# Group norm statistics inside the wkv7 loop, and another order of scores, maxima and norms in the attention of a hybrid decoder layer

## The reference

```
# RWKV-7 branch: 8 heads of 64
y, wkv = wkv7_scan(wkv0, rh, decay, kh, vh, -kk, kk * ah)
mu  = mean(y, axis=-1);  var = mean(square(y - mu), axis=-1)       # per token and head
y = (y - mu) * rsqrt(var + RW_GN_EPS) * rw_ln_w + rw_ln_b
y = y + sum(rh * kh * rw_r_k, axis=-1) * vh                        # the bonus
y = y * g                                                          # g = sigmoid(gd) @ rw_g2

# differential attention: 4 heads, two softmax maps each, causal
p = softmax(where(k_pos <= q_pos, q @ k.T * 64**-0.5, -inf))       # two maps per head
o = (p[map 0] - lam * p[map 1]) @ v
```

## Time and profile before

| | us |
|---|---|
| median of three runs | 2958.01 |
| the profiled execution | 2952.79 |
| its span | 2951.1 |
| TensorE busy (21313 matmuls) | 2745.0, 93% |
| VectorE busy (1339 instructions) | 1361.3, 46% |
| ScalarE busy | 658.3, 22% |
| GpSimd busy | 257.1, 9% |

### The profile page before, as it was taken

The page is one execution under the profiler, slowest core; times in us unless marked ns, Lnnn a source line. Parts: engine busy times, 40 slices in busy tenths (PEclk is TensorE's granted clock), DMA queues, the critical chain, the costliest instruction groups (busy, mean ns, idle before and its releaser), DMA issues.

```text
span 2951.1 us, 51413 instructions
## 1 busy us (share of the span) xinstructions
PE 2745.0 (93%) x21313; PEld 2582.2 (87%) x21313; DVE 1361.3 (46%) x1339; ACT 658.3 (22%) x967; POOL 257.1 (9%) x250
## 2 busy tenths in 40 slices
PE   6999999999999999996776999669999999999998
PEld 6999999999999999993344889439999999999998
DVE  4332233233673788776553656475453322332334
ACT  4111111112311222323322232111221111111123
POOL 1000000000000232111002454100000000000000
PEclk8999999999999999997987999769999999999999
DMA  3111111111333456669534000104211111111112
GB/s 101 50 43 50 43 50 50 43 43 50 115 99 103 143 175 223 201 188 330 164 114 124 25 28 17 42 29 145 92 44 50 50 43 45 48 50 45 48 41 74
DMA packets 270203, 252.02 MB, mean 85 GB/s; under 512 B 20724, under 2 KB 216144, under 8 KB 269920
## 3 DMA queue, kind: packets, MB, share of 16 engines
q1 hardware_dynamic: 252960, 189.42, 21.5%
q0 software_dynamic: 16896, 60.33, 5.6%
q10 hardware_dynamic: 192, 0.07, 0.0%
HBM read 209.87 MB, written 39.90 MB: 85 GB/s over the span
## 4 chain that ended last, share of the span: by engine, by line
PE 85%; DVE 9%; ACT 2%; issue 1%; DMA 1%; SPq 0%; DVEq 0%; POOL 0%; POOLq 0%; ACTq 0%
PE ps L1670 71%; DVE small L1438 1%; ACT probs L1022 1%; PE ps L1974 1%; PE ps L1989 1%; PE ps L1693 1%; PE ps L1994 1%; DVE rstd L1583 1%; PE ps L1714 1%; PE ps L1896 1%; PE ps L2001 1%; PE ps L1911 1%; PE ps L1834 1%; PE ps L2021 1%; PE ps L2029 1%
## 5 line engine op out<-in xcount | busy, mean ns | idle before, releaser
L1670 PE MATMUL ps<-h_hi,w_hi 128*128 128x344 f32 x3072 | 991.7, 323 | 10.3 <-DVE w_lo L1160 10.3
L1670 PE MATMUL ps<-h_lo,w_hi 128*128 128x344 f32 x3072 | 980.6, 319 | 0.0
L1670 PE MATMUL ps<-h_hi,w_lo 128*128 128x344 f32 x3072 | 980.3, 319 | 0.0
L1670 PEld LDWEIGHTS ps<-h_hi,w_hi 128*128 128x128 f32 x3072 | 577.8, 188 | 25.9 <-issue 19.8
L1670 PEld LDWEIGHTS ps<-h_lo,w_hi 128*128 128x128 f32 x3072 | 577.9, 188 | 2.1 <-issue 1.9
L1670 PEld LDWEIGHTS ps<-h_hi,w_lo 128*128 128x128 f32 x3072 | 577.9, 188 | 0.0
L1670 PE MATMUL ps<-ff_hi,w_hi 128*128 128x344 f32 x1056 | 337.1, 319 | 0.0
L1670 PE MATMUL ps<-ff_lo,w_hi 128*128 128x344 f32 x1056 | 336.6, 319 | 0.0
L1670 PE MATMUL ps<-ff_hi,w_lo 128*128 128x344 f32 x1056 | 336.2, 318 | 0.0
L810 ACT ACTIVATE w_hi<-w_stage 128x1024 fp32r<-128x1024 f32 x194 | 203.8, 1051 | 479.9 <-PE ps L1670 479.9
L1160 DVE TENSOR_TENSOR w_lo<-w_stage,w_hi 128x1024 fp32r<-128x1024 f32 x194 | 239.3, 1233 | 139.4 <-ACT w_hi L810 103.8
(11 more groups left out here) (388 smaller groups left out, 3219.1 us busy)
## 6 DMA issues: line engine op xcount, KB each, us to landing
w_stage<-in_ffn_up SPq DMA_DIRECT2D x176, 256.0 KB, 3.1
key_ring<-in_cache_k SPq DMA_DIRECT2D x128, 256.0 KB, 3.0
value_ring<-in_cache_v SPq DMA_DIRECT2D x128, 256.0 KB, 3.0
w_stage<-in_w_in SPq DMA_DIRECT2D x84, 256.0 KB, 3.3
w_stage<-in_ffn_down SPq DMA_DIRECT2D x80, 256.0 KB, 2.9
gate_save<-tmp POOLq DMA_DIRECT2D x16, 516.0 KB, 4.5
gate_ring<-gate_save POOLq DMA_DIRECT2D x16, 516.0 KB, 4.2
row_ring<-row_save SPq DMA_DIRECT2D x40, 128.0 KB, 2.9
```

Source lines behind the costliest of these rows:

```text
L1670: last = mm(dense[s][:, j], w[w0][:, k0 + k, :], r[:, k, j * CH:(j + 1) * CH], start=(k == 0 and n == 0), stop=(k == nk - 1 and n == 2))
```

## The change

**Group norm.** The mean is taken out before the outputs are formed: each of the three left operands of the output sums (state, values, solution) is centred over its 64 columns, so that y comes out centred. Its square is taken at once, and per chunk eight products with two columns of weights give, as token rows of each head, the variance and the bonus sum r k r_k; these are finished on 128 to 136 columns at a time. After the loop one root over all tokens follows, and each double head gets three parts: the two rows spread to 128 partitions, and the gate.

**Attention.** In steps 0 to 15 (n up to 512) the scores of a step use banks 0 and 1 (one map each) or 2 and 3, in turn, so they wait for the exponentials two steps back; VectorE takes the maxima of step s+1 ahead of the norm of step s. In steps 16 to 31 the mask, the maxima and the scaling are done map by map, and ScalarE waits for each map by itself.

```
# constants: one more table, (partition % 32 == column // 64), for the spread of two rows
+    put("row_heads", (s % 32 == t // 64) * 1.0)

# attention
+        def score_at(step, m):
+            return m * 512 + step % 2 * 1024 if step < 4 * HP else m * 1024
# ScalarE, probs(step)
-                act.wait_ge(*ev.at("neg_max", step + 1))
                 if step >= 2:
                     act.wait_ge(*ev.at("o_done", step - 1))
                 for m in range(2):
+                    act.wait_ge(*ev.at("neg_max", 2 * step + m + 1))
+                    b = score_at(step, m)
...
# VectorE, maxima(step)
+                for ms in ((0, 1),) if step < 4 * HP else ((0,), (1,)):
...
             maxima(0)
             for step in range(STEPS):
                 qi, s = step // HP, step % 2
                 n = (qi + 1) * P
+                if step + 1 < 4 * HP:
+                    maxima(step + 1)
                 dve.wait_ge(*ev.at("probs_made", 2 * step + 2))
...
-                if step + 1 < STEPS:
+                if 4 * HP <= step + 1 < STEPS:
                     maxima(step + 1)
# TensorE, scores(step)
-                pe.wait_ge(*ev.at("probs_made", 2 * step))
+                if step >= 2:
+                    pe.wait_ge(*ev.at("probs_made", 2 * step if step >= 4 * HP else 2 * step - 2))

# wkv7 loop: GpSimd, behind first_masks(c)
+            def bonus_products(c):
+                cols = slice(c * C, NT if c == NC - 1 else (c + 1) * C)
...
+                nc.gpsimd.tensor_tensor(Kf[:, :, cols], Rf[:, :, cols], Kf[:, :, cols], ALU.mult).then_inc(ev["ck_rk"], 1)
# ScalarE, behind ck_y
-                    sc.activation(CUM[:, :, p * C:(p + 1) * C], Y_PS, ACT.Copy).then_inc(ev["ck_y_out"], 1)
+                    sc.activation(CUM[:, :, p * C:(p + 1) * C], Y_PS, ACT.Copy)
+                    sc.activation(Bf[:, :, p * C:(p + 1) * C], Y_PS, ACT.Square).then_inc(ev["ck_y_out"], 1)
# VectorE, in next_state(p)
+                if p + 1 < NC:
+                    mean = mean8[:, 0:HP]
+                    in_turn(v.tensor_reduce(mean, new, AX, ALU.add))
+                    in_turn(v.scalar_tensor_tensor(Sc[(p + 1) % 2], mean.unsqueeze(2).broadcast_to([P, HP, 64]), -1.0 / 64, new,
+                                                   ALU.mult, ALU.add).then_inc(ev["ck_sc"], 1))
+            def centred_values(c):
+                dve.wait_ge(*ev.at("ck_tok_moved", 3 * c + 1))
+                in_turn(v.tensor_reduce(mean8, vtok.rearrange("p h (x n) -> p (h x) n", x=2), AX, ALU.add))
+                mean = mean8.rearrange("p (h x) -> p h x", h=HP).unsqueeze(3).broadcast_to([P, HP, 2, 64])
+                in_turn(v.tensor_scalar(mean8, mean8, 1.0 / 64, None, ALU.mult))
+                in_turn(v.tensor_tensor(Bf[:, :, c * C:(c + 1) * C].rearrange("p h (x n) -> p h x n", x=2),
+                                        vtok.rearrange("p h (x n) -> p h x n", x=2), mean, ALU.subtract).then_inc(ev["ck_vc"], 1))
+            def centred_solution(p):      # the same for Us (waits for ck_u_moved), written to KKn
...
+            def token_rows(p):
...
+                dve.wait_ge(*ev.at("ck_rows", p + 1))
+                in_turn(v.tensor_scalar(Rf[:, 0, cols], PS[:, 7, 0:n], 0.0, GN_EPS, ALU.max, ALU.add))
+                in_turn(v.tensor_copy(Rf[:, 1, cols], PS[:, 7, n:2 * n]).then_inc(ev["ck_rows_in"], 1))
+                in_turn(v.reciprocal(Rf[:, 0, cols], Rf[:, 0, cols]).then_inc(ev["y_inverse"], 1))
# VectorE, the loop over c
                 if c < NC:
                     level_sums(c, 1)
+                if c:
+                    centred_solution(p)
+                if c < NC:
                     level_sums(c, 2)
                 if c:
                     next_state(p)
+                    token_rows(p)
...
                     in_turn(v.tensor_tensor(heads8(arb), heads8(ABR_PS), wide("incl"), ALU.mult).then_inc(ev["ck_arb"], 1))
+                    centred_values(c)
# TensorE, outputs(p): reads Sc, the centred values and the centred solution, waits for ck_sc, ck_vc, ck_uc
+            def token_rows(p):
...
+                for h in range(HP):
+                    mm(PS[32 * h:32 * h + 2, 7, 0:n], row_scale, Bf[:, h, cols], start=True, stop=True)
+                for h in range(HP):
+                    last = mm(PS[32 * h:32 * h + 2, 7, n:2 * n], row_bonus[:, h], Kf[:, h, cols], start=True, stop=True)
+                last.then_inc(ev["ck_rows"], 1)
# TensorE, the loop over c
                 lower_products(c, 3)
                 if c + 1 < NC:
                     blocks(c + 1)
+                if c:
+                    token_rows(p)
                 level_products(c, 3)
+                if c:
+                    pe.wait_ge(*ev.at("ck_rows_in", c))
                 turn(c, 0, Vf[:, :, c * C:(c + 1) * C])

# after the loop, ScalarE
+            act.wait_ge(*ev.at("y_inverse", NC))
+            sc.activation(Rf[:, 0, :], Rf[:, 0, :], ACT.Sqrt).then_inc(ev["y_root"], 1)
             for h in range(HP):
...
+                act.wait_ge(*ev.at("y_used", 3 * h + 3))
+                sc.activation(YA[0][:, h, :], CUM[:, h, :], ACT.Copy).then_inc(ev["ya_high"], 1)
# after the loop, VectorE (in place of L1573 to L1593)
+            for h in range(HP):
+                y, t1, part = CUM[:, h, :], T[:, h % 2, :], 3 * h
+                dve.wait_ge(*ev.at("y_parts", part + 1))
+                in_turn(v.scalar_tensor_tensor(ch3(y), ch3(y), param("rw_ln_w", h), dense[part % 2], ALU.mult, ALU.mult)
+                        .then_inc(ev["y_used"], 1))
+                dve.wait_ge(*ev.at("y_parts", part + 2))
+                in_turn(v.tensor_tensor(ch3(t1), ch3(Vf[:, h, :]), dense[(part + 1) % 2], ALU.mult).then_inc(ev["y_used"], 1))
+                in_turn(v.scalar_tensor_tensor(y, y, param("rw_ln_b", h), t1, ALU.add, ALU.add))
+                if h:
+                    ya_low(h - 1)
+                dve.wait_ge(*ev.at("y_parts", part + 3))
+                in_turn(v.tensor_tensor(ch3(y), ch3(y), dense[part % 2], ALU.mult).then_inc(ev["y_used"], 1))
+            ya_low(HP - 1)
# after the loop, TensorE (in place of the column sums)
+            for part in range(3 * HP):
+                h, kind = divmod(part, 3)
+                if part >= 2:
+                    pe.wait_ge(*ev.at("y_used", part - 1))
...
+                q = slice(32 * h, 32 * h + 2)
+                for j in range(NCH):
+                    cols = slice(j * CH, (j + 1) * CH)
+                    if kind < 2:
+                        last = mm(dense[part % 2][:, j], K("row_heads")[q], Rf[q, kind, cols], start=True, stop=True)
+                    else:
+                        last = mm(dense[part % 2][:, j], G2[:, h * P:(h + 1) * P], gd[:, cols], start=True, stop=True)
+                last.then_inc(ev["y_parts"], 1)
```

More of the change, by code:

```diff
@@ L337, in build @@
         Pb = per_head(C + 1)
+        Sc = [per_head(64) for _ in range(2)]
+        mean8 = work(8)
+        row_scale = work(2)
+        row_bonus = work(2 * HP).rearrange("p (h x) -> p h x", h=HP)
         cumx = cum.rearrange("p (c n) -> p c n", c=NC)
@@ L755, in _ @@
             first_masks(0)
+            bonus_products(0)
             for c in range(NC):
@@ L1432, in maxima @@
                 n = (qi + 1) * P
[L1433 removed]
                 dve.wait_ge(*ev.at("scores_done", step + 1))
[L1435 to L1439 removed]
+                for ms in ((0, 1),) if step < 4 * HP else ((0,), (1,)):
+                    a, k = ms[0], len(ms)
+                    b = score_at(step, 0)
+                    scores = PSf[:, b:b + 1024].rearrange("p (m n) -> p m n", n=512)[:, :, 0:n] if k == 2 else \
+                        PSf[:, a * 1024:a * 1024 + n].unsqueeze(1)
+                    diag = scores[:, :, qi * P:n]
+                    in_turn(v.tensor_tensor(diag, diag, K("causal").unsqueeze(1).broadcast_to([P, k, P]), ALU.add))
+                    top = small[:, 24 + 2 * s + a:24 + 2 * s + a + k]
+                    in_turn(v.tensor_reduce(top, scores, AX, ALU.max))
+                    in_turn(v.tensor_scalar(small[:, 16 + 4 * s + a:16 + 4 * s + a + k], top, -SCALE, None, ALU.mult)
+                            .then_inc(ev["neg_max"], k))
             maxima(0)
@@ L1536, in state_step @@
                 if part == 8:
-                    in_turn(v.tensor_reduce(ysam[:, h, :], stm, AX, ALU.add))
+                    in_turn(v.tensor_reduce(ysam[:, h, :], stm, AX, ALU.add).then_inc(ev["y_sample"], 1))
+            in_turn(v.memset(Sc[0], 0.0).then_inc(ev["ck_sc"], 1))
+            in_turn(v.tensor_scalar(row_scale, heads, 1.0 / 64, None, ALU.mult))
+            in_turn(v.tensor_tensor(row_bonus, heads.unsqueeze(1).broadcast_to([P, HP, 2]), bc(param("rw_r_k", 0, HP).unsqueeze(2), 2),
+                                    ALU.mult))
             blocks(0)
@@ L1895, in scores @@
                         w = min(512, n - j)
-                        last = mm(PSf[:, m * 1024 + j:m * 1024 + j + w], Q[q, h, qi * P:n], Kr[q, h, j:j + w],
```

(2 more changed lines are left out.)

120 lines of the change are left out of this document (59 added, 61 removed).

## The result

The changed kernel takes 2967.76 us (median of six runs, 2964.25 to 2968.82) against 2955.88 for the kernel before (six runs, 2950.56 to 2962.52): a ratio of **1.0038**, 95% interval 1.0023 to 1.0053. It is slower by about 0.4%, just over what a measurement of this kernel can tell. The forecast was 2956 and "the same" the likeliest of the three; 2967.8 lies inside the range of 2932 to 2977, in the part that was given to "slower". The profiled execution took 2968.71 us, 15.9 more than that of before.

A forecast was written before the change was run, and what follows sets the result against it. TensorE bounds the large products and the loop, engine-to-engine chains the attention and group norm. Terms -52.7 + 10 + 44 - 3.5 = -2.2 gave 2950.6 us profiled, 2956 as median; range 2932 to 2977.

The forecast's parts named there:

- Group norm, -52.7: Group norm after the loop: twelve parts at half clock take 43.0 us, start moves +0.4, replacing 96.1 us.
- the 29 at high clock: Group norm: at high clock VectorE's 6.6 us a head would decide, the stretch 29 us, a change of -66.
- Loop, +10.4 with the start of the norm: wkv7 loop: added token rows delay TensorE 1.05 us a chunk, +10 in all; norm start adds 0.4.
- second rival: wkv7 loop: VectorE's added 6.4 us a chunk exceeds its idle time and delays TensorE; 2979 us, chance 0.22.
- Short steps, +44: Attention steps 0 to 15: the new order makes steps longer, +44 us, between +32 and +56.
- the ring: Short steps: weights, transposes, copy, values product, page product, scores, maxima, norm in sequence; 8.5 us against 5.4 at 512 columns.
- Then the clock: Short steps: TensorE's idle lowers its clock, adding 1.2 us a step for steps 8 to 14, 8.4 together.
- low for all of a step: Short steps, upper end: the clock stays low throughout a step, +56 us.
- Long steps, -3.5: Attention steps 16 to 31: map-by-map maxima release probabilities earlier, saving 3.5 us, between 0 and 8.

The follow-up runs named there:

- rows_scalar: norm_only with the token rows' copy moved to ScalarE and VectorE's floor and reciprocal moved to the chunk's end; 2904.63 us, 0.9837 of before.
- filler: Changed kernel plus two unused fp32 products of 384 columns on TensorE in steps 4 to 14, before its wait for the weights; 2950.35 us, 0.9993 of before.
- two_ahead: Changed kernel with TensorE issuing short-step scores two steps ahead, early maxima kept, long steps as before the change; 2913.47 us, 0.9869 of before.
- banks_alone: norm_only with short-step scores in the two bank pairs in turn, maxima still behind the norm; 2915.55 us, 0.9877 of before.
- norm_only: Changed kernel with the whole attention put back as before, keeping the group norm and loop part; 2914.87 us, 0.9875 of before.

## Why the prediction was wrong

**Group norm, -52.7: right.** The stretch took 42.02 where 43.0 was worked out, at half clock for the most part. The half clock was the choice that counted: the 29 at high clock would have been 13 off.

**Loop, +10.4 with the start of the norm: right in its mechanism, 2.8 short.** It is the token rows ahead of the level 3 sums: 1.33 a chunk and not 1.05; and twice the clock fell behind the longer wait at L2079, 1.5 each, which the sum had no term for. rows_scalar, where that wait is 1.01 to 1.44 in the last five chunks, has neither fall; a filler in the loop, which would test the clock by itself, wasn't run. (The second rival's 6.4 a chunk for VectorE's added work is 6.1 by the prediction's own parts, which changes nothing.) The second rival's condition (VectorE's idle time before L1491 used up) didn't come: it shrank from 3.54 to 1.70 and from 2.82 to 0.67. The eight narrow products in four strips took 0.55, where sixteen records as wide take 1.16. By the Trainium skill ("TensorE: Matmul & The Clock Gate", Part 3) small outputs in different strips run at the same time; the row agrees.

**Short steps, +44: this step failed.** The order of the ring was right in each link, and filler, two_ahead and banks_alone confirm it from three sides. What failed is the term "Then the clock. [...] I add 1.2 a step for steps 8 to 14, 8.4": the short steps cost 52.4 (0.4 and 52.0), near the upper end of 56 named as "low for all of a step". Steps 4 to 7, priced in part from rows at half clock, were put at 31.6 and took 30.8. Steps 8 to 14 were priced from rows at high clock, 57.5 with the turned sums, and took 75.6: 18.1 more, 2.6 a step, for which 1.2 a step had been added. And those 1.2 are the difference of one group only, the scores of the earlier trace rows at either clock. But in a ring nothing runs beside TensorE's links, so each of its four groups of products pays in full: in the step shown above they took 6.1 us instead of 3.7, and that is the whole of what this step was over. TensorE's idle before the transposes (3.50 in that step), behind which they ran slow, comes in every step because of the ring itself. filler took 9.2 of the 18.1 away at a granted clock of 0.82; how much of the other 8.9 is still the clock isn't separated. The half clock of the steps with 256 columns, in the order of before, could have been the warning for the wider ones.

**Long steps, -3.5: wrong in sign, +1.1, and +3.0 behind them.** From step 19 on the gain is there, 1.8 (117.36 to 115.52), half of what was taken. The seam was costed at nothing. Step 16 is the first whose maxima stand behind the norm again, and it took 1.9 more, waiting for late scores; step 18 took 1.2 more at a lower clock, as it does in norm_only without a seam. Behind the last step, the 3.0 weren't named at all; waits for pages stand there, but their share is not shown.

The terms that missed by more than 1: clock of the short steps +9.8, seam and long steps +4.6, end of the attention +3.0, loop +2.8. They all have one sign (the attention up to step 3 and the group norm, 1.0 each, have the other), and since a gain of 53 and a loss of 54 were set against each other, their sum decided the sign of the result.

## What to carry to other kernels

When a wait becomes part of a ring through TensorE, price the ring at half clock first, all of its products and not one, and only then ask what could hold the clock up; here filling the idle time with unused products gave 13 us back. An operation moved ahead in one engine's queue gains nothing while what it waits for stands where it was in another's: move the producer first (two_ahead), then the consumer. Where a small operation is added to a busy chain, its place can cost more than its length: with two of the three operations at the end of the chunk and the copy on ScalarE the loop gave 5.6 us back, more of it by the clock than by the shorter waits.

## What was not expected of the hardware

- A wait of TensorE that was only 0.6 to 1 us longer than before (2.02 against 1.03 to 1.45) was followed by products at half clock, twice in the last five chunks of the changed kernel (granted clock 0.95 over each of these two, 1.00 over the other three). In norm_only it happened behind 1.62 and 2.21, but not behind the 2.02 of two other chunks; in the last five of rows_scalar, where that wait was 1.01 to 1.44, never.
- VectorE's operation on 8 columns, 0.17 us alone, took 0.41 in the changed kernel (L1558) and, in two_ahead (L1559), 0.81. Both ended 0.03 us behind the end of GpSimd's product beside them (1708.65 + 1.27, and 1717.47 + 1.27). The changed kernel has sixteen such operations (L1549, L1558): six with no GpSimd operation beside them took 0.17 each, and the ten others 0.23 to 0.96, each ending within 0.04 us of the end of GpSimd's. The timelines of the changed kernel and of two_ahead:

```profile
1708.65 1.27 POOL L750 TENSOR_TENSOR chunk_work<-chunk_work,loop_masks 128x512 f32<-128x512 f32 x1 [3.21 <-PE ps L2046]
...
1709.54 0.41 DVE L1558 TENSOR_SCALAR chunk_work<-chunk_work 128x8 f32<-128x8 f32 x1
```

```profile
1717.47 1.27 POOL L750 TENSOR_TENSOR chunk_work<-chunk_work,loop_masks 128x512 f32<-128x512 f32 x1 [2.81 <-PE ps L2050]
...
1717.96 0.81 DVE L1559 TENSOR_SCALAR chunk_work<-chunk_work 128x8 f32<-128x8 f32 x1
```

The Trainium skill, in "SBUF — State Buffer" ("Who interferes with whom"), says that the port pair the two engines share is held for a whole instruction and that the other engine is blocked meanwhile; these rows agree, down to an operation of 8 columns.
